# A two-block transformer kernel on one core: two fixed expert pairs ahead of the routing, the shared expert in plain f32, the router by token block

## The reference, cut to what matters

```python
def moe_ffn(xt, w_router, router_bias, w_gate_e, w_up_e, w_down_e, w_gate_sh, w_up_sh, w_down_sh):
    scores = jax.nn.sigmoid((xt @ w_router).astype(jnp.float32))      # 256 tokens x 64 experts
    choice = scores + router_bias                                     # 4 of 8 groups, then 8 of 64 experts
    ...
    wts = wts / jnp.sum(wts, axis=-1, keepdims=True) * ROUTED_SCALE
    ...
        ye = swiglu(xt[rows], w_gate_e[e], w_up_e[e], w_down_e[e]) * wr[:, None]
    ...
    return routed + swiglu(xt, w_gate_sh, w_up_sh, w_down_sh)         # the shared expert, every token
```

## Time and profile before

| | |
|---|---|
| median of 3 runs | 1341.66 us (1339.59 to 1341.88) |
| profiled execution: its own time | 1339.06 us |
| profiled execution: span of the trace | 1336.1 us |
| PE busy / PEld / DVE / ACT / POOL | 1217.5 / 844.7 / 553.5 / 451.6 / 45.7 us |
| HBM read | 355.37 MB, 269 GB/s over the span |
| mean granted TensorE clock | 0.954 |

### The profile page before, as it was taken

One profiled execution on the slowest core, in us unless ns is written; L12 is line 12 of the kernel. 1 busy time (PEld: TensorE's weight loads), 2 busy tenths in 40 slices (PEclk: granted clock), 3 DMA queues, 4 the chain that ended last, 5 costly groups with the idle time before them and its releaser, 6 DMA issues.

```text
span 1336.1 us, 16400 instructions
## 1 busy us (share of the span) xinstructions
PE 1217.5 (91%) x6541; PEld 844.7 (63%) x6544; DVE 553.5 (41%) x815; ACT 451.6 (34%) x656; POOL 45.7 (3%) x66
## 2 busy tenths in 40 slices
PE   5999998799899599889999769999989987899998
PEld 2877777674355244434444337888879866788886
DVE  1555546673022111112211155554456645544444
ACT  1345445341022111112212134333345544433333
POOL 0000000000000000000000020210010001000000
PEclk8899999899899899989999879999999978899999
DMA  9996655459999999999999996465615106355540
GB/s 370 351 365 223 233 202 165 182 205 412 387 422 420 393 422 420 421 391 421 421 421 420 421 283 193 167 203 187 231 57 190 63 1 221 132 198 186 186 146 31
DMA packets 115170, 359.51 MB, mean 269 GB/s; under 512 B 15077, under 2 KB 62614, under 8 KB 84063
## 3 DMA queue, kind: packets, MB, share of 16 engines
q1 hardware_dynamic: 113376, 352.71, 69.8%
q0 software_dynamic: 320, 3.46, 0.6%
q10 hardware_dynamic: 1406, 2.42, 0.5%
HBM read 355.37 MB, written 4.50 MB: 269 GB/s over the span
## 4 chain that ended last, share of the span: by engine, by line
PE 82%; DMA 8%; DVE 5%; ACT 3%; issue 1%; SPq 1%; POOL 1%; DVEq 0%; POOLq 0%; ACTq 0%
PE bank L1965 30%; PE bank L2178 16%; PE bank L2105 9%; DMA ring<-in_w_up_e 6%; PE bank L2203 5%; PE bank L2052 4%; PE bank L2155 3%; PE bank L2215 3%; PE bank L1981 1%; PE bank L2270 1%; PE bank L2292 1%; DMA arena<-in_w_ada 1%; PE bank L2021 1%; SPq L588 1%; PE bank L2094 1%
## 5 line engine op out<-in xcount | busy, mean ns | idle before, releaser
L2178 PE MATMUL bank<-ring,xg 128*64 128x512 f32 (+1 forms) x1152 | 212.8, 638 | 40.8 <-DMA ring<-in_w_up_e 40.8
L1965 PE MATMUL bank<-g_hi,xt_hi 128*128 128x512 f32 (+1 forms) x592 | 239.9, 405 | 5.8 <-DVE xt_lo L1881 2.2
L1256 DVE TENSOR_TENSOR g_lo<-raw_g,g_hi 128x2048 fp32r<-128x2048 f32 (+2 forms) x86 | 197.2, 2295 | 114.5 <-ACT g_hi L804 57.8
L1965 PE MATMUL bank<-g_hi,xt_lo 128*128 128x512 f32 (+1 forms) x592 | 232.7, 393 | 0.0
L1965 PE MATMUL bank<-g_lo,xt_hi 128*128 128x512 f32 (+1 forms) x592 | 232.1, 392 | 0.0
L2178 PEld LDWEIGHTS bank<-ring,xg 128*64 128x64 f32 (+1 forms) x1152 | 66.1, 133 | 184.1 <-issue 184.0
L1965 PEld LDWEIGHTS bank<-g_hi,xt_hi 128*128 128x128 f32 x592 | 112.9, 191 | 35.6 <-issue 10.2
L1965 PEld LDWEIGHTS bank<-g_hi,xt_lo 128*128 128x128 f32 x592 | 112.4, 190 | 24.1
L1965 PEld LDWEIGHTS bank<-g_lo,xt_hi 128*128 128x128 f32 x592 | 112.9, 191 | 21.2
L804 ACT ACTIVATE g_hi<-raw_g 128x2048 fp32r<-128x2048 f32 (+3 forms) x42 | 78.2, 1865 | 78.3 <-PE bank L1965 40.1
L1401 DVE SCALAR_TENSOR_TENSOR arena<-arena,w_row_of,bank 128x256 f32<-128x256 f32 x28 | 13.4, 480 | 218.4 <-ACT arena L924 214.3
(11 more groups left out here) (364 smaller groups left out, 1613.0 us busy)
## 6 DMA issues: line engine op xcount, KB each, us to landing
ring<-in_w_gate_e SPq DMA_DIRECT2D x64, 1024.0 KB, 12.3
ring<-in_w_up_e SPq DMA_DIRECT2D x64, 1024.0 KB, 16.4
ring<-in_w_down_e SPq DMA_DIRECT2D x64, 1024.0 KB, 15.6
raw_g<-in_ffn_w_gu SPq DMA_DIRECT2D x44, 1024.0 KB, 8.3
raw_g<-in_w_in SPq DMA_DIRECT2D x26, 1024.0 KB, 7.5
raw_d<-in_ffn_w_down SPq DMA_DIRECT2D x22, 1024.0 KB, 5.0
ada_d<-in_w_ada SPq DMA_DIRECT2D x16, 1024.0 KB, 6.7
raw_g<-in_w_out SPq DMA_DIRECT2D x8, 1024.0 KB, 5.3
```

The costliest lines, as they stand in the source:

```text
L1256: dve.tensor_tensor(lo, raw, hi.bitcast(F32), ALU.subtract).then_inc(S.lo_g, 1)
L1965: last = pe.matmul(out_, src[s][:, c, b * P:(b + 1) * P], w((g_hi, g_lo)[m], i), start=start and i == 0 and k == 0, stop=stop and i == len ...
L2178: last = pe.matmul(bank(4)[r, :].rearrange("p (g n) -> p g n", g=2), xg[:, s // 2 % 2, c, at_:at_ + r.stop - r.start], gate_up_raw(pair, j ...
```

## The change

1. The first four places of the order go to experts 63, 62, 61 and 60 (FIRST_SMALL = 4). SP loads both pairs ahead of the routing, slot 0 behind the `lo_g` of G_WO + 1 and slot 1 behind its `used_g`. After `ordered` it goes on with turn 2.
2. The shared expert has memory of its own (`g_sh`, `d_sh`) and is multiplied in plain f32 from the transposed tokens `tok_t`. Its feed-forward width is taken in two halves k, each by token block b: (0, 0) before and between the steps of the routing, (0, 1) at turn 2, turn and down of half 0 at turn 3, (1, 0) and (1, 1) at turn 8, turn and down of half 1 at turn 9.
3. The router is multiplied in f32 with tokens on the partitions, block by block. The scores need no turn back.
4. The token parts for the gather are made right after the norm, in h's own layout; `fill` reads every eighth element of them as weights. The picks of turns 0 and 1 come from `rows_in` (`pick_first`), before the order is known; the four first fills stand before the tables are brought into order, and ACT alone empties them.
5. `rows_beyond` and `rows_of_big` now come behind `row_weight(0)`, which waits for `pick_t(0)`, and that has moved behind turn 0's gate and up.
6. pre1 is loaded just before ff1's first group, post1, mixpre and mixpost after the tables of neighbourhood attention; only final_g stays ahead of the experts.

```diff
@@ the turn table and the jobs
-FIRST_SMALL, FIRST_BIG, N_SMALL = 2, 60, 20
+FIRST_SMALL, FIRST_BIG, N_SMALL = 4, 60, 20
...
+SH_PE = {(0, 0): 1, (0, 1): 2, 0: 3, (1, 0): 4, (1, 1): 5, 1: 6}
+SH_WAITS = {(0, 0): 1, (0, 1): 2, (1, 0): 5, (1, 1): 5}
+SH_TURNS = (2, 8)
@@ sync: loads
-            gated_stream(M, G_SH, D_SH, 1, lambda s, it: (a["w_gate_sh"][0], a["w_up_sh"][0]),
-                         lambda s, it: a["w_down_sh"][0])
-            for dst, n in ((final_g, "final_g"), (pre1, "ffn1_pre_g_2"), (post1, "ffn1_post_g_2"),
-                           (mixpre, "mix_pre_g_2"), (mixpost, "mix_post_g_2")):
...
-            sp.wait_ge(M.lo_g, 2 * G_SH + 2)
-            load_gate_up(0, (0, 1))
-            sp.wait_ge(M.lo_d, D_SH + 1)
-            load_pair_down(0, (0, 1))
-            sp.wait_ge(M.used_g, 2 * G_SH + 2)
-            sp.wait_ge(M.used_d, D_SH + 2)
+            for k, n in enumerate(("w_gate_sh", "w_up_sh")):
+                sp.dma_start(g_sh[:, k, :, :], a[n][0].rearrange("(p c) n -> p c n", c=DC)).then_inc(sh_in, 16)
+            sp.wait_ge(M.lo_g, 2 * (G_WO + 1) + 2)
+            load_gate_up(0, (E - 1, E - 2))
+            load_pair_down(0, (E - 1, E - 2))
+            sp.wait_ge(M.used_g, 2 * (G_WO + 1) + 2)
+            load_gate_up(1, (E - 3, E - 4))
+            load_pair_down(1, (E - 3, E - 4))
+            sp.wait_ge(in_["mods"], 512)
+            for k in range(2):
+                sp.dma_start(d_sh[k], a["w_down_sh"][0][k * P:(k + 1) * P, :]).then_inc(sh_in, 16)
+            sp.dma_start(final_g, a["final_g"].rearrange("(o n) -> o n", o=1).to_broadcast([P, D])).then_inc(in_["gains"], 16)
             sp.wait_ge(ordered, 1)
-            for _, places, load, _, _ in TURNS[1:]:
+            for _, places, load, _, _ in TURNS[2:]:
...
             sp.wait_ge(used_gu, 4 * N_TURN)
+            sp.dma_start(pre1, a["ffn1_pre_g_2"].to_broadcast([P, D])).then_inc(in_["gains"], 16)
...
+                for dst, n in ((post1, "ffn1_post_g_2"), (mixpre, "mix_pre_g_2"), (mixpost, "mix_post_g_2")):
+                    sp.dma_start(dst, a[n].to_broadcast([P, D])).then_inc(in_["post"], 16)
@@ scalar, ahead of the experts
+            act.wait_ge(M.used_g, 2 * (G_WO + 1) + 2)
+            tok_high(0)
+            tok_turned(0)
+            tok_turned(1)
+            tok_high(1)
+            scores(0)
+            tok_turned(2)
+            tok_turned(3)
+            scores(1)
+            sh_silu(0, 0)
             sparse_phase()
@@ vector
             link(route(0))
             route(1).then_inc(rt_sel, 1)
-            lo_down(D_SH)
-            gate(M, 0, 0)
+            tok_rest(1)
             dve.wait_ge(rt_pos, 1)
...
             ins.then_inc(rt_sel, 1)
-            lo_gated(D_SH)
+            dve.wait_ge(rt_sel, 2)
+            pick_first()
             dve.wait_ge(rt_pos, 2)
...
-                gathered(1)
-                gathered(3)
+                pick_rows(1)
                 row_weight(0)
-                pick_rows(1)
                 rows_beyond()
                 rows_of_big()
@@ tensor: jobs of the shared expert
+            def sh_chunks(k, b, cs):
+                for c in cs:
+                    last = pe.matmul(sh_bank(b).rearrange("p (g n) -> p g n", g=2), tok_t[:, c, b * P:(b + 1) * P],
+                                     g_sh[:, :, c, k * P:(k + 1) * P], start=c == 0, stop=c == DC - 1)
+                return last
...
+            def sh_down(k):
+                pe.wait_ge(sh_act, SH_PE[k])
+                for b in range(TB):
+                    for m in range(2):
+                        pe.matmul(bank(2 * b + m), sh_t[:, b, :], d_sh[k][:, m * 512:(m + 1) * 512], start=False, stop=False,
+                                  skip_group_check=True)
@@ fill
-                                last = pe.matmul(fill_bank(n)[:, i * 4 * ROWS:(i + 1) * 4 * ROWS], tok[k][:, b, c, :],
+                                last = pe.matmul(fill_bank(n)[:, i * 4 * ROWS:(i + 1) * 4 * ROWS], tok[k][:, b, c:D:DC],
@@ body
                         else:
                             pe.wait_ge(xg_first, 4)
+                            pe.wait_ge(sh_dve, 1)
                     if s:
                         pe.wait_ge(sp_gate, s)
+                    if s == SH_TURNS[0]:
+                        sh_gate_up(0, 1)
+                        pe.wait_ge(sh_dve, 2)
+                    if s == SH_TURNS[1]:
+                        sh_gate_up(1, 0)
+                        sh_gate_up(1, 1)
+                        pe.wait_ge(sh_dve, 4)
+                    if s - 1 in SH_TURNS:
+                        pe.wait_ge(xg_sb, 2 * s)
+                        sh_turn(SH_TURNS.index(s - 1))
+                        sh_down(SH_TURNS.index(s - 1))
                     rows_gate_up(s)
+                    if s == 0:
+                        pick_t(0)
@@ tensor, from the router to turn 0
+            pe.wait_ge(in_["wrt"], 16)
+            for b in range(TB):
+                transposes(2, qs=(2 * b, 2 * b + 1))
+                for u in range(2):
+                    pe.wait_ge(M.xt_hi, 8 + 2 * b + u + 1)
+                    for c in range(4 * u, 4 * u + 4):
+                        last = pe.matmul(score_bank(b), tok_t[:, c, b * P:(b + 1) * P], w_rt[:, c, :],
+                                         start=c == 0, stop=c == DC - 1)
+                last.then_inc(rt_ps, 1)
             zero_sums().then_inc(M.used_d, 1)
-            gate_up(M, G_SH, 0, 0)
-            gate_up(M, G_SH, 0, 1)
+            pe.wait_ge(sh_in, 64)
+            sh_chunks(0, 0, range(6))
             pe.wait_ge(rt_sel, 1)
...
+            last.then_inc(rt_pos, 1)
+            sh_chunks(0, 0, range(6, DC)).then_inc(sh_pe, 1)
             pe.wait_ge(rt_sel, 2)
...
+                pe.wait_ge(M.xt_lo, 12)
                 for n in range(4):
                     fill(n)
-                pe.wait_ge(xg_first, 4)
-                pick_t(0)
+                pe.wait_ge(rt_sel, 3)
+                pe.matmul(bank(7)[0:1, P:P + E], od[low, 1:2], place[low, low], start=True, stop=True)
+                pe.matmul(bank(7)[:, 0:P], by_expert[:, 0:P], place[:, :], start=True, stop=True)
+                pe.wait_ge(xg_first, 3)
+                pe.matmul(bank(5)[:, 0:P], by_expert[:, P:2 * P], place[:, :], start=True, stop=True).then_inc(rt_pos, 1)
                 for s in range(N_TURN):
                     body(s)
@@ launch
-    nc = bacc.Bacc("TRN2", target_bir_lowering=False, num_devices=1)
+    nc = bacc.Bacc("TRN2", target_bir_lowering=False, num_devices=1, dynamic_dma_scratch_size=4096)
```

More of the change, by code:

```diff
@@ L59 @@
 G_WO = G_WB + 2
-G_SH = G_WO + 2
-G_FF1 = G_SH + 1
+G_FF1 = G_WO + 2
 G_WIN2 = G_FF1 + N_FF
@@ L228, in build @@
         past_cap, w_past = rt[:, 2 * E:4 * E], rt[:, 4 * E:6 * E]
-        score_t = rt[0:E, 12 * E:16 * E]
         w_over = area(34, TB * E).rearrange("p (b e) -> p b e", b=TB)
         rbias = area(35, E)
-        w_rt_hl = [t[:, :, :].rearrange("p c t -> p (c t)").rearrange("p (c e) -> p c e", c=DC) for t in (at_hi, at_lo)]
-        final_g, pre1, post1 = area(36, D), area(40, D), area(44, D)
+        g_sh = area(40, 2 * UNIT).rearrange("p (g c n) -> p g c n", g=2, c=DC)
+        d_sh = (area(36, D), d_sh1[:, :])
+        a_sh, silu_sh = ([t[:, 1, b * P:(b + 1) * P] for b in range(TB)] for t in (a_sb, silu))
+        pre1, post1 = area(40, D), area(44, D)
         mixpre, mixpost = area(48, D), area(52, D)
@@ L404, in build @@
             EV_A[g], EV_V[g] = n_a, n_v
-        PHASES = {"sh": (M, G_SH, D_SH, 0, 1), "over": (OV, 0, 0, 0, E), "ff1": (M, G_FF1, D_FF1, 1, N_FF),
-                  "ff2": (M, G_FF2, D_FF2, 1 + N_FF, N_FF)}
+        PHASES = {"over": (OV, 0, 0, 0, E), "ff1": (M, G_FF1, D_FF1, 0, N_FF),
+                  "ff2": (M, G_FF2, D_FF2, N_FF, N_FF)}
         HALVED = (4, 9, 11)
@@ L931, in body @@
                         gathered(2 * s + 5)
+                for n in range(4):
+                    gathered(n)
                 act.wait_ge(rt_pos, 3)
-                by_place = bank(6)[:, 0:P].rearrange("p (b e) -> p b e", b=TB)
+                by_place = bank(5)[:, 0:P].rearrange("p (b e) -> p b e", b=TB)
                 small_end = FIRST_SMALL + 4 * N_QUAD
@@ L1115, in _, with tok_high, tok_turned, scores @@
                 square_rows(1, b, x[:, b, :])
-            split_hi(G_SH, 0, True)
-            transposed(2)
-            split_hi(G_SH, 1, True)
-            act.wait_ge(rt_ps, 1)
-            act.activation(score_t, bank(7)[0:E, 0:T], ACT.Sigmoid).then_inc(rt_sc, 1)
-            hi_down(D_SH)
-            act.wait_ge(M.used_g, 2 * G_SH + 2)
-            for b in range(TB):
-                act.activation(silu[:, b, :], bank(4 + b)[:, 0:FF], ACT.Silu).then_inc(M.silu_done, 1)
+            def tok_high(b):
+                act.wait_ge(h_ready, 4 + b + 1)
+                act.activation(tok[0][:, b, :], h[:, b, :], ACT.Copy).then_inc(tok_hi, 1)
+            def tok_turned(q):
+                act.wait_ge(M.xt_ps, 8 + q + 1)
```

(20 more changed lines are left out.)

169 lines of the change are left out of this document (81 added, 88 removed).

## The result

The changed kernel takes **1374.86 us** (median of 4 runs, 1374.06 to 1375.60) against 1340.62 us before (4 runs): ratio **1.0256**, 95% interval 1.0238 to 1.0274, so 34 us slower. Forecast were 1335.8 us and a range of 1324 to 1345; what happened is rival (c), priced at 1382 us.

What follows compares the result with a forecast made beforehand. Transfers set the pace between Q turns, so the queue's early start and its empty time around Q turns count. Terms -4.6 + 2.3 - 2.8 - 2.4 + 1.6 = -5.9 us took 1341.66 to 1335.8; range 1324 to 1345.

Steps and rivals of the forecast that it cites:

- rival (c): Gather fills: weights at stride double a fill, 1.03 us more in 52 fills, PE sets the pace, 1382 us; chance 0.10.
- So I charge nothing: Gather fills: reading weights at every eighth element costs no extra, as transposes of h at that stride take 0.12 us each.
- Start: Routing to turn 0: counting starts 4.0 us later behind `sh_in`, yet turn 0's gate and up ends 4.6 us earlier.
- Rows_beyond: Behind turn 0's product: DVE's counting now delays PE's turn to 3.8 us after the product, from 1.5; +2.3 us.
- Turn 2: Shared expert's job fits PE's idle, gate and up takes 7.0 us instead of 9.79, pair 4 issued earlier; -2.8 us.
- Turn 8: Shared expert's jobs about fill PE's idle, gate and up takes 7.0 us instead of 8.58; -2.4 us.
- Exit: Before ff1: pre1 now stands on the chain ahead of ff1's first group; +1.6 us, bounds +0.5 and +2.
- The preload of pair 1: Transfer queue: loading the second pair early is worth nothing itself, since pair 3 must wait for turn 1's gate and up.
- Jobs hidden at waits: Turns 2, 3, 8, 9: shared expert's jobs about fit PE's idle; without idle they would cost 3.5 to 8 us each.
- Rival (a): Before the counting: the wait on `sh_in` does not bind, 11 us more are gained, 1325 us; chance 0.14.
- Rival (b): Turns with jobs and start: the gains at the clock fail, the start stays at half clock, 1343 us; chance 0.20.
- It is wrong if ... a fill takes over 1.3 us: Sign in the new trace against the forecast, which expected gather fills at 1.0 to 1.15 us.

Runs made afterwards that it cites:

- e2: The kernel before with one edit, the gather's weights at every eighth element: 1369.92 us, ratio 1.0224 to the kernel before.
- e1: The changed kernel with token parts stored chunk by chunk, so the gather reads its weights contiguous: 1339.17 us, ratio 0.9997 to the kernel before.
- e7: e4 with pre1 loaded in the middle of the experts instead of ahead of ff1's first group: 1322.82 us, ratio 0.9886 to the kernel before.
- e3: e1 with the shared expert's first chunks waiting only for their own two transfers: 1328.14 us, ratio 0.9913 to the kernel before.
- e5: e3 with pair 1 loaded only after the order is known: 1327.27 us, ratio 0.9916 to the kernel before.
- e6: e3 with the shared expert's jobs at turns 4 and 10 instead of 2 and 8: 1347.50 us, ratio 1.0061 to the kernel before.
- e4: e3 with the counting of lost rows put ahead of row_weight(0) on DVE: 1324.62 us, ratio 0.9912 to the kernel before.

## Why the prediction was wrong, point by point

**The fills at a stride: the step that failed.** "So I charge nothing" rested on the earlier trace rows: transposes of h, at the same stride of eight elements, 0.12 us each. Rows of the other kind stood beside it: ACT pays twice for that stride. The fill's products do pay: eight of them take 2.13 and 1.91 us instead of 1.15 and 0.95. The error was to take the pace of one kind of instruction, a transpose with 128 moving columns, for another, an f32r product with 256, because both load weights at the same stride.

And the transposes were not free of it either; 0.12 us was compared with a fill's product and not with a contiguous transpose. Contiguous transposes of h at full clock are in the trace of e2 (L1991). The loads at eight elements, below, are those of the earlier trace rows, also at full clock, and L2094 of e2 loads another tile at two elements. Behind the busy time stands the mean in ns; the middle row has the shortest, median and longest load in ns:

```profile
L1991 PEld LDWEIGHTS bank<-con,h_tok 128*128 128x128 f32 x16 | 1.7, 140 | 0.0
...
L1952 PEld LDWEIGHTS bank<-con,h_tok x8: 185/194/207, 230.0 to 230.8; 128*128 128x128 f32 x8
...
L2094 PEld LDWEIGHTS bank<-con,arena 128*128 128x128 f32 x92 | 14.5, 203 | 1.8
```

A contiguous load takes 140 ns, one at eight elements 194 (the median), at two elements 203 on average; this last row is of another stage and so the weaker one. The loads follow one another at 0.11 us (1.73 us for 16) and 0.12 us, so hardly any of the 54 ns shows in the pace. For the gather's loads the extra is 149 ns, and the pace doubles. Why the two kinds differ, and why two elements are nearly free for the one kind and not for the other, no run separates. The mechanism had stood as rival (c), at 0.10, and its price for a fill holds well: 52 fills, 0.97 us more in each or 50.4, and 3.9 more in the four first ones (7.70 against 3.81 in e1), 54.3 in all. Of that, 35.7 reached the end (1374.86 - 1339.17). The other 18.6 did not: PE's idle time within the span is 13.5 us less than in e1 (102.2 against 115.7), and the rest is PE's other work, which takes less time, in part because fewer products follow a wait and run at a lowered clock. The rival had counted 8 us of room. It also subtracted 6 us for the forecast's gain, which wasn't there, and started from 1341.66 instead of the 1339.17 of e1. So 10.6 us too little room, 6 us too much gain and 2.5 us too high a start make up the 7 us between 1382 and 1374.86; that the rival comes out so near is in part luck.

**Where the forecast's own 5.9 us went.** e1 is the kernel that the forecast had described. It came out 0.4 us faster than before by its ratio (1.9 faster to 1.1 slower) instead of 5.9. The chains of both show where. Before:

```profile
302.59 7.02 PE bank L2178 x32
...
312.65 3.58 PE bank L2203 x16
316.23 6.92 PE bank L2178 x32
...
763.36 9.52 PE bank L2178 x64
```

e1:

```profile
254.97 3.19 PE bank L2010 x14
...
263.58 23.93 DMA d_sh<-in_w_down_sh
...
299.96 7.02 PE bank L2253 x32
...
310.28 0.49 DVE arena L1455
...
311.32 0.97 PE bank L2228 x8
312.29 5.21 PE bank L2278 x16
317.49 6.92 PE bank L2253 x32
...
338.28 7.07 PE bank L2253 x64
...
761.95 9.22 PE bank L2253 x64
...
772.26 10.85 DMA raw_g<-in_ffn_w_gu
```

In this execution of e1 the last product of W_OUT ends at 258.16, before at 256.81. Kernels that are alike up to there lie between 255.72 (e7) and 258.33 (e3), so that is chance, and I measure from there:

| us after the last product of W_OUT | before | e1 | difference |
|---|---|---|---|
| end of turn 0's gate and up | 52.8 | 48.8 | -4.0 |
| start of turn 1's | 59.4 | 59.3 | -0.1 |
| end of turn 2's | 89.1 | 87.2 | -1.9 |
| end of the last turn's | 516.1 | 513.0 | -3.1 |
| ff1's first landing | 524.6 | 524.9 | +0.3 |

- **Start: -4.6 forecast, -4.0 measured.** The wait on `sh_in` binds as it was said: in the changed kernel, the last shared transfer lands at 286.45 (forecast 285.4), and the six chunks take 4.84 us, 4.6 were taken. Right, a bit mis-sized.
- **Rows_beyond: +2.3.** Turn 0's gate product starts 3.3 us behind PE's product and PE goes on at 3.8 (306.98 to 310.81), the very figure forecast. Right.
- **Left out: +1.6.** PE then does turn 0's down product partly at half clock, 5.21 us for 16 products, where the kernel before takes 3.58. The mean granted clock from 312.3 to 317.5 is 0.69, in the kernel before 1.00 in the same product. I had seen what the clock takes at turns 2 and 3, but not asked whether my own new gap of PE, behind a cool start, would cost the same. With this, -4.0 + 2.3 + 1.6 = -0.1: the whole gain of the start is gone before turn 1.
- **Turn 2: -2.8 forecast, -1.8 measured.** The product is 7.07 us instead of 9.79, as forecast. But the transfer for it takes 13.6 us from issue to landing (324.56 to 338.15), where it took 12.7. Ahead of that issue nothing had been transferred from 320 to 324.5; before, the transfers ran at 417 GB/s until the issue. That this gap costs the 0.9 us is likely and not shown. In the changed kernel the issue of pair 4 is at 349.71, not near 341; in e1 at 345.62.
- **Turn 8: -2.4 forecast, -1.5 measured** (-3.4 against -1.9: its product ends at 450.91 in e1 and 452.97 before). Later turns shift by 0.3 us back.
- **Exit: +1.6 forecast, +3.4 measured at the landing.** From the end of the last product to ff1's landing are 11.9 us instead of 8.6. I had priced pre1 by the spacing of the old gain rows. Here it stands alone ahead of a group that ACT waits for, and costs twice that. e7 takes it away from there and gets back to 8.7, though its median gains only 1.8 us.
- **The preload of pair 1, worth nothing:** right (e5). **Jobs hidden at waits:** right (e6). **Rival (a)**, that the wait on `sh_in` doesn't bind, wasn't so, but what it would be worth was 11 us, and e3 measured 11.0. **Rival (b)** wasn't so either: in e1 the products of turns 2 and 8 took 7.07 and 7.17 us, so the gains at the clock were there.

The terms as measured, -4.0 + 2.3 + 1.6 - 1.8 - 1.5 + 0.3 + 3.4, come to +0.3, which is e1. So without the stride there would have been no change that can be measured, inside the forecast's range but 5.5 us short of its gain: the sum of the other terms was mis-sized as well. The stride alone made the kernel slower.

**What the forecast said would show.** "It is wrong if ... a fill takes over 1.3 us" was the sign that appeared, with 2.13. Turn 0's product ended at 309.79 instead of 305, DVE had finished `route(1)` at 278.65 instead of 276, and turn 2's product was at 7.07 as forecast.

**Left open.** Why turn 0's down product is partly at half clock in e1 and not in e3, which has the same gap of PE ahead of it: in e1, PE had stood idle for some 10 us before its chunks and worked them off largely at half clock, in e3 it had not. No run separates the one from the other. Not tried were the shared expert's down transfers ahead of pair 0 and e7 with pair 1 loaded late.

## What to carry to other kernels

A layout that saves a copy once may be read many times: here, two copies at a stride became contiguous, which spared some 2.2 us of ACT (4.29 against twice 1.06), and each of 52 half gathers paid 0.97 us for it. To learn what an access pattern costs, compare an instruction with the same kind of instruction without the pattern. Where two rows of a trace disagree, give the case against the forecast more than a tenth. And when a wait covers several transfers, wait only for those that the next instruction reads: that was worth 11 us here, more than the whole gain that was forecast.

## What the runs showed of the hardware that was not expected

- The load of 128 weights of an f32r product takes 189 ns contiguous, 196 at two elements, 330 at four and 338 at eight, and eight products of 256 columns go from 0.95 to 1.91 us. Plain f32 transposes pay less and with another step: 140 ns a load contiguous, 203 at two elements, 194 at eight, and still 0.12 us apart.
- A single row of 512 KB, spread to all partitions, ahead of a group of weights delays its landing by 3.4 us (e1 against the kernel before) and 3.2 us (e4 against e7); the time for its bytes at 421 GB/s is 1.2 us, an estimate.
- The same 16 products took 5.21 us in e1 and 3.58 in e3, behind the same gap of PE. What differs before them are the chunks before the counting, which e1 does after some 10 us of idle at a mean granted clock of 0.58, and e3 at 0.95. That this is the cause is not shown.
